# Half of the MLP's input by seven block products of eight, with its weight sums made in DRAM

## The reference, cut to what matters

```
h = rms_norm(x, pre_norm_mlp[l])                                  # 512 x 1024
y = jnp.square(jax.nn.relu(h @ w_mlp_in[l])) @ w_mlp_out[l]       # 1024 x 4096, 4096 x 1024
x = x + rms_norm(y, post_norm_mlp[l])
```

## Time and profile before

| what | value |
|---|---|
| median of 3 runs | 749.78 us (749.64 to 750.03) |
| profiled execution, its own time | 749.47 us |
| its span, first to last instruction | 747.9 us |
| PE busy in the span | 739.4 us (99%), 4168 matmuls |
| PE's weight loads busy | 607.1 us (81%) |
| DVE, ACT, POOL busy | 438.7, 389.4, 318.5 us (59, 52, 43%) |
| transfers | 129.21 MB, mean 173 GB/s |

### The profile page before, as it was taken

How to read it: one execution, slowest core, us unless ns; L and a number is a source line. 1 busy time by engine, 2 the same in 40 slices (tenths; PEclk the granted TensorE clock), 3 DMA queues, 4 the chain that set the end, 5 groups by cost and what they waited for, 6 DMA issues and landing times.

```text
span 747.9 us, 11901 instructions
## 1 busy us (share of the span) xinstructions
PE 739.4 (99%) x4168; PEld 607.1 (81%) x4168; DVE 438.7 (59%) x651; ACT 389.4 (52%) x632; POOL 318.5 (43%) x296
## 2 busy tenths in 40 slices
PE   9999999999999999999999999999999999999996
PEld 7788778888887878888878988888888888888885
DVE  5897899981444645345983512221221777778795
ACT  6657842268555364635645733333332655555671
POOL 2357894535444654564536464645645000000002
PEclk9999999999999999999999999999999999999999
DMA  9336124456366577266551279779887575654652
GB/s 340 104 95 202 57 81 104 127 128 186 117 158 155 196 163 208 69 150 214 206 170 28 85 241 293 191 259 286 194 275 204 153 234 196 195 189 151 216 177 113
DMA packets 52893, 129.21 MB, mean 173 GB/s; under 512 B 6096, under 2 KB 6512, under 8 KB 50544
## 3 DMA queue, kind: packets, MB, share of 16 engines
q1 hardware_dynamic: 49120, 109.47, 44.3%
q0 software_dynamic: 3392, 18.88, 13.1%
q10 hardware_dynamic: 336, 0.28, 0.1%
HBM read 126.49 MB, written 39.86 MB: 222 GB/s over the span
## 4 chain that ended last, share of the span: by engine, by line
PE 88%; DVE 4%; POOL 3%; ACT 2%; issue 1%; DMA 1%; SPq 0%; DVEq 0%; POOLq 0%; ACTq 0%
PE bank L758 27%; PE bank L759 26%; PE bank L760 26%; POOL rsq L2158 2%; PE bank L1005 1%; PE bank L1028 1%; PE bank L1015 1%; POOL w_lo L2164 1%; DVE bank L1884 1%; PE bank L969 1%; PE bank L933 1%; PE bank L788 1%; PE bank L980 1%; DMA raw<-in_w_out 0%; DVE w_lo L1638 0%
## 5 line engine op out<-in xcount | busy, mean ns | idle before, releaser
L2164 POOL TENSOR_TENSOR w_lo<-raw,w_hi 128x512 fp32r<-128x512 f32 x169 | 219.9, 1310 | 240.0 <-ACT w_hi L1220 238.2
L1220 ACT ACTIVATE w_hi<-raw 128x512 fp32r<-128x512 f32 (+2 forms) x214 | 145.1, 685 | 154.5 <-PE bank L760 118.7
L758 PE MATMUL bank<-h_hi,w_hi 128*128 128x512 f32 (+1 forms) x528 | 208.5, 395 | 0.2
L759 PE MATMUL bank<-h_lo,w_hi 128*128 128x512 f32 (+1 forms) x528 | 204.2, 387 | 0.0
L760 PE MATMUL bank<-h_hi,w_lo 128*128 128x512 f32 (+1 forms) x528 | 204.1, 386 | 0.0
L758 PEld LDWEIGHTS bank<-h_hi,w_hi 128*128 128x128 f32 x528 | 99.2, 188 | 25.8 <-issue 5.1
L760 PEld LDWEIGHTS bank<-h_hi,w_lo 128*128 128x128 f32 x528 | 99.2, 188 | 20.6
L759 PEld LDWEIGHTS bank<-h_lo,w_hi 128*128 128x128 f32 x528 | 99.3, 188 | 18.5
L1629 DVE SCALAR_TENSOR_TENSOR relu_sb<-bank,rs_row 128x512 f32<-128x512 f32 x32 | 20.6, 686 | 125.9 <-PE bank L760 114.2
L2302 POOL TENSOR_SCALAR ssh<-ssy 128x1 f32<-128x1 f32 x4 | 1.0, 238 | 151.6 <-ACT junk L1600 151.6
L758 PE MATMUL bank<-w_hi,a_hi 128*128 128x512 f32 x120 | 46.8, 390 | 0.0
(11 more groups left out here) (327 smaller groups left out, 1262.7 us busy)
## 6 DMA issues: line engine op xcount, KB each, us to landing
raw<-in_w_in SPq DMA_DIRECT2D x87, 256.0 KB, 2.7
raw<-in_w_mlp_in SPq DMA_DIRECT2D x62, 256.0 KB, 4.8
t_sum<-in_w_mlp_out POOLq DMA_DIRECT2D x12, 1024.0 KB, 9.4
raw<-in_w_mlp_out SPq DMA_DIRECT2D x26, 256.0 KB, 2.7
raw<-t_sum SPq DMA_DIRECT2D x26, 256.0 KB, 2.9
v_sum<-in_w_mlp_out POOLq DMA_DIRECT2D x4, 1024.0 KB, 9.4
raw_b<-in_w_mlp_out SPq DMA_DIRECT2D x16, 256.0 KB, 2.9
raw_b<-t_sum SPq DMA_DIRECT2D x14, 256.0 KB, 2.9
```

The costliest lines, as they stand in the source:

```text
L758: pe.matmul(o, s_hi, m_hi, start=start, stop=False, skip_group_check=True)
L759: pe.matmul(o, s_hi, m_lo, start=False, stop=False, skip_group_check=True)
L1220: return a.activation(o, i_, ACT.Copy, scale=scale)
L2164: g.tensor_tensor(w_lo[:, slot, :], raw[:, slot, :], w_hi[:, slot, :].bitcast(F32), ALU.subtract).then_inc(lo_ready, 1)
```

## The change

The first 8 groups of the MLP's input (2048 features, `G_PLAIN`) stay as they are. The other 2048 features are taken in 4 steps of 512 features, in two halves of 256, together with two halves of the 1024 input features and two halves of the 512 tokens: a 2 x 2 x 2 block product, done by seven products instead of eight. Each product takes 512 input features, 256 output features and 256 tokens: 2 units of 12 matmuls with 256 columns. A step has 14 units, and the low parts of units 1, 3, 7 and 11 are made by POOL, the others by DVE.

- Four of the seven products have a sum of weight blocks; the sums are made in DRAM in four kinds and two chunks of 1 MB (`u_copy`, `u_add`), placed from unit 48 on (`IN_SUM_AT`). The copies of the output's sums are moved back for that: two stay before the MLP, six lie in groups 2 to 7, four in the steps (`STEP_SUMS`), and the last kind in the output's sweeps, where SP issues them between calls of `one` and `two`. `copy_sum` waits for the add before of the same kind. The mixer's sums move a few units.
- Four products have a sum of token blocks: DVE makes four full blocks and four sums, ACT and DVE split them (`full_block`, `t_blocks_made`, `block_high`, `t_low`), during groups 4 to 8.
- The seven results are combined per step by DVE out of PSUM and three small tiles (`p1` copied by ACT, `e1`, `f1`), then ReLU (one of 256 and one of 768 elements for each of two rows), then squares one step later (`square_in`).
- In the steps a ring of 8 raw tiles replaces the 4.
- The token blocks lie where `x_res` and `pn_mlp` lay. SP copies the residual to DRAM in groups 2 and 3; in the output's sweeps POOL fetches it back tile by tile, and `pn_mlp` with it.

Cut to its core:

```diff
-U_M1 = U_OUT + 64
+G_PLAIN = 8
+F_HALF = (FF - G_PLAIN * 256) // 2
+U_S = U_OUT + 4 * G_PLAIN
+STEPS_IN = F_HALF // 256
+PER_STEP = 14
+RING = 8
+CHUNKS = F_HALF // 512
+U_M1 = U_S + STEPS_IN * PER_STEP
...
-OUT_SUM_AT = {48: 0, 52: 1, 60: 2, 87: 3}
+OUT_SUM_AT = {61: 0, 70: 1, 73: 2, 88: 3}
...
-SUM_AT = {61: (0, 0), 65: (1, 0), 73: (2, 0), 74: (0, 1), 78: (1, 1), 86: (2, 1)}
+SUM_AT = {82: (0, 0), 85: (1, 0)}
...
-SUM_IN = {2: (0, 2), 3: (0, 3), 4: (3, 0), 5: (3, 1), 7: (2, 2), 8: (2, 3), 9: (1, 2), 10: (1, 3), 12: (3, 2), 13: (3, 3)}
+IN_SUM_AT = {48: (0, 0), 51: (0, 1), 55: (1, 0), 58: (1, 1), 64: (2, 0), 67: (2, 1), 76: (3, 0), 79: (3, 1)}
...
+SUM_IN = {2: (2, 0), 3: (0, 1), 4: (1, 1), 5: (0, 2), 6: (2, 1), 7: (1, 2)}
+STEP_SUMS = {(0, 8): (0, 3), (1, 4): (2, 2), (2, 4): (1, 3), (3, 0): (2, 3)}
...
+IN_PRODUCTS = ("q1", "q6", "q5", "q2", "q7", "q3", "q4")
+IN_BANK = {"q1": 0, "q2": 0, "q6": 2, "q7": 2, "q4": 2, "q5": 4, "q3": 4}
+LOW_POOL = (1, 3, 7, 11)
```

SP:

```diff
+        def copy_sum(q, i, sources=N_SUM):
+            sp_.wait_ge(*added(q, i))
+            if q > 1:
+                sp_.wait_ge(*added(q - 2 if q == 2 else 2, sources))
+            sp_.dma_start(*t_copy(q, i)).then_inc(t_copied[q], 16)
...
+                if g in (2, 3) and j % 2:
+                    t = 2 * (g - 2) + j // 2
...
+                    sp_.dma_start(x2_copy[t], x_res[:, t, :]).then_inc(copied_out, 16)
             if g in SUM_IN:
...
+                copy_sum(*SUM_IN[g], 1 if g == 2 else 2)
+        for s in range(STEPS_IN):
+            for v in range(PER_STEP):
+                u = U_S + PER_STEP * s + v
+                if v >= RING - RAW or s:
+                    sp_.wait_ge(*low_of(u - RING))
+                sp_.dma_start(raw_of(u), in_source(s, v)).then_inc(raw_signal(u)[0], 16)
+                if (s, v) in STEP_SUMS:
+                    copy_sum(*STEP_SUMS[s, v], 3 + s // 3)
...
-        with sp_.Fori(2, NI) as i:
-            one(i)
...
+        one(2)
+        copy_sum(3, 0)
+        one(3)
+        one(4)
+        copy_sum(3, 1)
...
```

PE, one product of a step:

```diff
+            for half in range(2):
+                u = U_S + PER_STEP * s + 2 * IN_PRODUCTS.index(name) + half
+                pe.wait_ge(*low_of(u))
+                for kk in range(2):
+                    for e in range(2):
+                        c = slice(kk * 256 + e * P, kk * 256 + e * P + P)
+                        x_ = three(bank[IN_BANK[name] + e][:, 0:256], w_hi[:, u % SPL, c], w_lo[:, u % SPL, c],
+                                   *in_operand(name, 2 * half + kk), name in ("q1", "q6", "q5") and half + kk == 0,
+                                   name in ("q2", "q4", "q3") and half + kk == 2)
```

ACT in a step and at the border to the output:

```diff
+                if v == 2:
+                    if s:
+                        a.wait_ge(made_in, made("c21", s - 1, 1))
+                    for e in range(2):
+                        copy(p1[:, e, :], bank[e][:, 0:256]).then_inc(p1_copied, 1)
+                if s and v in (3, 4):
+                    square_in(s - 1, v - 3)
+                if s == STEPS_IN - 1 and v == 8:
+                    a_split(0, 0, slice(0, 4))
...
         a_split(1, 1, slice(0, 4))
-        square_group(NI - 1, 1)
         w_split(6, 2, 16)
+        for e in range(2):
+            square_in(STEPS_IN - 1, e)
```

DVE: each pair of results waits for its product, and `combine` stands at v = 7 and 9; the border:

```diff
+        for s in range(STEPS_IN):
+            step_in(s)
+        w_low(2, 1, 3)
+        v.wait_ge(unit_done, U_M1)
+        for e in range(2):
+            c21(STEPS_IN - 1, e)
         w_low(3, 1, 4)
         w_low(4, 2, 6)
         a_low(1, 1, slice(0, 4), 2)
+        for e in range(2):
+            relu_in(STEPS_IN - 1, e)
         w_low(6, 2, 8)
```

POOL, behind the steps:

```diff
+        for t, q_i in ((0, (3, 0)), (1, (3, 1)), (2, None), (3, (3, 2))):
+            g.wait_ge(part_done, (24, 32, 48, 56)[t])
+            g.dma_start(x_res[:, t, :], x2_copy[t]).then_inc(late_in, 16)
+            if q_i:
+                add_sum(*q_i)
+        g.dma_start(pn_mlp[:], post_norm_mlp[0].partition_broadcast(P)).then_inc(late_in, 16)
+        add_sum(3, 3)
```

More of the change, by code:

```diff
@@ L187, in loads, with made @@
     return u // 4 + 1 - (1 if u >= U_X and u % 4 >= 2 else 0)
+def made(name, s, e):
+    return 14 * s + 2 * ("e1", "f", "c11", "c22", "c12", "c21", "relu").index(name) + e + 1
 STEPS = side_steps()
@@ L723, in _ @@
         one(1, range(2, 8))
[L724 to L726 removed]
+        for q in range(3):
+            sp_.wait_ge(*added(q, N_SUM))
+        one(2)
[3 more added lines that the diff above has]
+        copy_sum(3, 1)
+        one(5)
+        one(6)
+        copy_sum(3, 2)
+        one(7)
         two(0, S_TWO - 8)
@@ L730, in _ @@
             part(s, w2_rows(s + 8, 1, 1))
-        with sp_.Fori(1, 5) as i:
-            two(i, i * 6 + (S_TWO - 6))
+        two(1, S_TWO)
+        copy_sum(3, 3)
+        two(2, S_TWO + 6)
+        two(3, S_TWO + 12)
+        two(4, S_TWO + 18)
         sp_.wait_ge(end_lo, 3)
@@ L1162, in one @@
                     pe.wait_ge(part_lo, i * 8 + (s + 1))
-                    if first and p == 0 and c > 1:
-                        pe.wait_ge(relu_done, 30 if c == 2 else 32)
+                    if first and p == 0 and c != 1:
+                        pe.wait_ge(made_in, made({0: "c12", 2: "c11", 3: "c21"}[c], STEPS_IN - 1, 1))
                     for i2 in range(2):
@@ L1494, in mlp_in @@
                     a.wait_ge(row_full, 1)
-                    mark(copy(rs_row[:], bank[7][:]), row_ready)
+                    mark(copy(rs_row, bank[7][:]), row_ready)
+                    mark(copy(rs_ext[:, 0:256], bank[7][:, 256:512]), row_ready)
                     square_group(i, 0)
-                if last and j >= 5:
-                    if j == 5:
-                        a_split(0, 0, slice(0, 4))
-                    a.wait_ge(unit_done, U_M1 + j - 8)
-                    w_split(j - 5, 1, 16)
-                elif not (first and j < 3):
+                if not (first and j < 3):
@@ L1503, in mlp_in, with block_high, split_in @@
                     split(None, u % 4, i * 32 + 16 * loads(u), i * 8 + (u - 3))
-                if j == 3 and not first or j == 7 and not last:
+                if j == 3 and not first or j == 7:
                     square_group(i, j // 4)
+        def block_high(n_):
+            a.wait_ge(diffs_made, OUT_G + n_ + 1)
+            if n_ == 0:
+                a.wait_ge(copied_out, 16 * (1 + NT))
+            b = T_ORDER[n_]
+            copy(ts_hi[b][:], t_full[b][:]).then_inc(dhi_ready, 1)
+        def split_in(u):
+            a.wait_ge(*raw_signal(u))
+            a.wait_ge(unit_done, u - 3)
+            copy(w_hi[:, u % 4, :], raw_of(u)).then_inc(hi_ready, 1)
@@ new lines, in mlp_in_last, with square_in @@
+        def mlp_in_last(i):
+            for j in range(8):
+                u = U_OUT + LEAD + 8 * i + j
+                if u < U_S:
+                    split(None, u % 4, 16 * loads(u), u - 3)
+                else:
+                    split_in(u)
+                if j in (3, 7):
+                    square_group(i, j // 4)
+                if j in (2, 3, 4, 5):
+                    block_high(j - 2)
+        def square_in(s, e):
+            a.wait_ge(made_in, made("relu", s, e))
+            for m in range(2):
+                a.activation(act_pair(G_PLAIN + 2 * s + e, slice(4, 6) if m else slice(0, 3, 2)),
+                             relu_sb[:, 2 * e + m, :].rearrange("p (s c) -> p s c", s=2), ACT.Square).then_inc(act_ready, 1)
@@ L1517, in _ @@
         mlp_in(0, True)
-        with a.Fori(1, 7) as i:
+        with a.Fori(1, 3) as i:
             mlp_in(i, False)
-        mlp_in(7, False, True)
+        mlp_in_last(3)
+        for s in range(STEPS_IN):
+            mlp_in_step(s)
         def one(i, last=False):
@@ L1993, in relu @@
                     v.wait_ge(act_ready, i * 4 + (m + 1 - 4))
-                stt(relu_sb[:, m, :], bank[4 + m if first and m < 2 else m][:], 0.0, rs_row[:], ALU.max, ALU.mult).then_inc(relu_done, 1)
+                stt(relu_sb[:, m, :], bank[4 + m if first and m < 2 else m][:], 0.0, rs_row, ALU.max, ALU.mult).then_inc(relu_done, 1)
         def combine(n):
@@ new lines, in _ @@
+        relu(0, True)
+        relu(1, ms=(0, 1))
+        combine(0)
+        relu(1, ms=(2, 3))
+        combine(1)
+        relu(2, ms=(0, 1))
+        combine(2)
+        for b in range(4):
+            full_block(b)
+        relu(2, ms=(2, 3))
+        combine(3)
+        t_blocks_made()
+        relu(3, ms=(0, 1))
+        combine(4)
+        for i in range(4):
+            t_low(i)
+        for u in range(U_S, U_S + LEAD):
+            in_low(u)
+        relu(3, ms=(2, 3))
+        combine(5)
```

279 lines of the change are left out of this document (224 added, 55 removed).

## The result

The changed kernel takes 760.77 us (median of 4 runs, 759.33 to 761.27), the kernel before 749.83 beside it: ratio 1.0142, interval 1.013 to 1.0153. It is 1.4% slower, where 745.8 us was forecast, with a range from 743.2 to 749.8; "slower" had been given a chance of 0.11. The profiled execution took 760.39 us, its span is 758.7.

What follows compares the result with a forecast made beforehand. PE, busy 739.4 of 747.9 us, was taken as the bound, with DMA nearly used up: 749.47 - 6.5 (PE) + 1.7 (border) + 0.8 (DMA) = 745.5, plus 0.3 for the median: 745.8 us, range 743.2 to 749.8.

Steps and rivals of the forecast that it cites:

- The PE term: MLP's input: 384 matmuls of 512 columns (87.0 us) become 672 of 256 (80.5 us), a gain of 6.5 us.
- Weight loads don't overlap: Rival, steps: 672 weight loads at 0.188 us take 126 us instead of 80.5, some 791 us in all; chance 0.02.
- the change doesn't save: Rival, steps: start-based prices hide gaps, 256-column units run at 0.13 us a matmul, 750 to 752 us; chance 0.04.
- Side work before unit 90: Rival: side work there slips behind later loads, costing 1 to 4 us, 747 to 750 us; chance 0.08.
- The steps' order: Order of work within a step: the tightest wait, q4's for c22, holds with 0.5 us to spare; nothing was charged.
- The sum of the DMA work: From 425.5 us to the MLP's output, loads, copies, adds and residual make 155 of 157 us; 0.8 us charged.
- the bound: Upper bound on the DMA loss: 6 us, if each MB on q1 costs 3.06 us, as after 588 us.
- What protects PE is lead: Steps: a load may take 11.5 us to land before PE stops; the longest landing seen beside an add is 10.9.
- the token blocks to stop q6 if late: Token blocks, made in groups 5 to 8, would if late stop product q6 of step 0; DVE and ACT had room.
- it is within the 0.8: Output's first sweep: 6.4 us of loads plus about 5 us of sums in 10.9, covered by the 0.8 us charged.
- loads starve in the steps or in the first sweep: Rival: 2 to 8 us lost, 747 to 753 us, at v = 8 to 14 of steps 0 and 3; chance 0.24.
- The border: Start of the MLP's output: DVE's a_lo ready at M+12.6, PE wants it at M+10.9; 1.7 us stall (1.0 to 2.6).

Runs made afterwards that it cites:

- e1: Changed kernel without the copies and adds of the MLP output's weight sums; its products read plain blocks: 748.28 us, ratio 0.9977.
- e3: Changed kernel without the output's sums, and with the last relus and squares behind the work for the output's second pass: 746.23 us, ratio 0.9957.
- e5: Changed kernel, same bytes: three output-sum copies and adds before the MLP input's first group, fourth-kind copies and adds earlier, residual fetches behind part 70: 751.5 us, 1.0018.
- e7: Changed kernel with only the later half of e5's reorder: fourth-kind copies and adds earlier, residual fetches behind part 70: 752.94 us, ratio 1.0046.
- e10: Changed kernel with the edits of e5 and e2, the three early copies 12 us earlier still, their adds between the mean squares: 748.49 us, ratio 0.9986.
- e12: Changed kernel without the residual's round trip through DRAM (four writes, four fetches), all sums in place: 751.94 us, ratio 1.0028.
- e14: Changed kernel without the residual's four writes to DRAM; the fetches read the kernel's input x instead: 757.5 us, ratio 1.0108.
- e13: e10 without the residual's round trip through DRAM (four writes, four fetches): 748.87 us, ratio 0.9977.
- e4: Changed kernel with eight extra matmuls of 512 columns into a free bank in front of step 0: 759.62 us, ratio 1.0122.
- e15: Changed kernel with only the residual's four fetches moved, behind parts 70 to 88 and the last add: 757.97 us, ratio 1.0119.
- e11: Changed kernel with one POOL loop changed: the first three fourth-kind adds ahead of the residual's fetches instead of between them: 764.31 us, ratio 1.02.
- e2: Changed kernel with the last relus and squares behind the work for the output's second pass: 757.93 us, ratio 1.013.

## Why the prediction was wrong

The profiled executions side by side:

```
                    step 0    M       last    M to last   median
before              502.2     589.21  741.52  152.3       749.8
after               505.20    587.39  752.40  165.0       760.8
e1 no sums          502.32    582.95  740.28  157.3       748.3
e3 and border       502.67    583.30  737.30  154.0       746.2
e5 head + tail      504.66    585.29  743.74  158.5       751.5
e7 tail             507.62    589.51  746.54  157.0       752.9
e10 early + border  503.66    584.29  739.88  155.6       748.5
e12 no residual     502.53    583.15  743.86  160.7       751.9
e14 no writes       502.75    584.10  749.01  164.9       757.5
```

- **The PE term was right.** 672 matmuls took 80.63 us in e1, e3 and e5, 0.1200 us each, and M moved by 6.26 where nothing was late. "Weight loads don't overlap" and "the change doesn't save" are out. By the rule of the Trainium skill (TensorE: Matmul & The Clock Gate, section "The mechanism") quoted in the prediction, these steps would have taken 126 us; the trace disagrees here too. The prediction left out that the same section of the Trainium skill also names a load into the background weight buffer as one that is pulled ahead; no run shows which buffer is used.
- **Side work before unit 90 didn't slip**: the first product with 512 columns starts at 425.74 us, before at 425.51. The steps' order held: in the changed kernel no wait for `p1` or `relu_sb` of the steps, in other runs at most 1.1 us.
- **The sum of the DMA work was near, its price was not.** 155 us of work in 157 was forecast. From 425 to 587 us the two queues were busy 91.3% of 162 us, 148 us, with windows of 1.02 and 1.05 in the steps. But the sums cost 12.5 us (after less e1) where 0.8 was taken and 6 was the bound. The step that failed is "What protects PE is lead": it set one landing, 10.9 us, against 11.5 of lead. With both queues full, the loads before step 0 took 14.0 us. They had been issued 16.4 us before PE wanted them (486.66 and 503.11), more than the 11.5; but from the landing to the product lay 4.7 us, where the sum had 2.1, since `ts_hi` and `ts_lo` stood in between. The prediction expected the token blocks to stop q6 if late; they stood ahead of the first unit's `w_lo`. No run moves them, so their share of the 1.93 us is not shown; e1, e12 and e14, with the same order and earlier landings, have no stop there. Against the bound: it priced the bytes that don't fit; what PE loses is the lateness of the one load that it needs next, and the bytes stay the same (e7, e10).
- **The output sweep was the larger half, and it was waved through**: "it is within the 0.8", "POOL is idle in that stage, so fetching the residual blocks nobody". POOL's engine is idle, but its queue stood 43.76 us at part 24, and the add that SP needs stood behind it. The prediction named what queues behind SP's waits and not what queues behind POOL's. Moving adds and fetches took 7.8 us off (e7). The stop at 708.74 needed no landing beyond 10.9: its load took 10.98 us. PE wanted the product at 705.4, and 2.55 us lay from the landing to the product, so that only 7.6 us were left for the landing in this execution. The prediction worked out a lead for the first sweep (12.7 us) and none for the second.
- **Order and bytes are not two shares that add up.** Order alone gives 9.3 us (e5), 4 MB alone 8.8 (e12), and with the order mended the 4 MB give nothing (e13). My reading, which fits these runs and which none tests by itself: a queue at its limit passes lateness on until a gap in the traffic ends it; either a gap or fewer bytes does. The rival "loads starve in the steps or in the first sweep" came nearest: one stop lies at the first sweep's end (648.72). It had the place wrong otherwise (v = 8 to 14 of steps 0 and 3, where PE never stopped in the changed kernel), and with 2 to 8 us the size.
- **The border** was forecast at 1.7 us (1.0 to 2.6) and is 2.41 in the changed kernel, 2.69 in e1, at M + 13.5 and M + 14.2: the mechanism is right, the term is 0.7 to 1.0 short. In the changed kernel ACT nearly keeps the sum's times (squares done at M + 8.5, `a_hi` at M + 11.3); what the sum left out is a low part of 1.22 us (`w_lo`, 598.39) that DVE makes ahead of `a_lo`. In e1 ACT also stood 3.28 us for the load of `raw_c`, and the squares began at M + 7.0. And with what follows the stop it costs more: M to last is 5.0 us longer in e1 and 1.7 in e3.
- **A term was missing: the clock behind a stop.** About 4.8 us of the changed kernel (three times 1.6). e4 shows the first of them: PE kept busy, clock full, steps 1.3 us shorter.

What stays open: when the clock falls behind a stop, and why executions of one kernel differ so much once stops depend on transfers: 0.1% for the kernel before (0.3% at most, beside e12), 1.3% in e15. Several profiled executions lie off their median for this reason (e4, e11, e13). So e15's part rests on its trace alone.

## What to carry to other kernels

When a kernel's queue of transfers is to be filled to the last per cent, price the load that the engine needs next, not the bytes: list every request that stands ahead of it in each queue, with the semaphore that each waits for, on the issuing engines that look idle too. A request that waits for one thing must not stand ahead of one that another queue waits for. Then look for stretches in which the transfers rest and move sums there, before counting on the engine's saving: here the same bytes took 751.5 us (e5) or 764.3 (e11) by their order alone.

## What the runs showed that was not expected

- A stop of TensorE may cost again as much by the granted clock, or not. Behind 1.93 us (505 us), 2.41 and 2.42 us in the changed kernel it was 0.57 to 0.61; behind 3.19 us at 708.74 it was 1.00. In e2 a stop of 3.21 us was followed by 0.62 and one of 2.28 by 1.00; in e4 the stop of 2.69 us at the border by 0.50, in e14 one of 2.69 by 1.00. e5 and e7 have stops of 2.45 and 2.57 us, and 1.00 behind them. What decides between them the rows don't show.
- Loads of 256 KB land in 3.5 us (e1, no sums beside them, median), 7.2, 8.6 and 14.0 us, by what is in the queues; at DMA shares from 480 to 500 us of 0.45, 0.99, 0.97 and 0.89: the share doesn't tell the last three apart.
